# Three feed forwards: the down projection by seven products of halves, with the sums of weight blocks on GpSimd

## The chip, the core and the metric

The program runs on one core of one Trainium2 chip. The metric is the device time of one execution in microseconds (us), the median of several runs.

## What is computed

A sequence of 512 rows of width 1024 goes through three transformer layers in float32: one with a gated spatial branch and dilated attention, one with latent attention (MLA), one with an mLSTM. Each layer ends in a feed forward of width 4096 with a squared relu. The change concerns these three alone:

```python
n2 = rms_norm(h, norm_mlp_pre[l])                                        # first layer
hid = jnp.square(jax.nn.relu(jnp.einsum('bsd,df->bsf', n2, w_up[l])))    # 1024 -> 4096
mlp_out = jnp.einsum('bsf,fd->bsd', hid, w_down[l])                      # 4096 -> 1024
h = h + rms_norm(mlp_out, norm_mlp_post[l])
...
x = x + sqrelu_mlp(rms_norm_2(x, norm_ffn[i]), ffn_w1[i], ffn_w2[i])     # second and third
```

## The kernel before

**Products in three parts.** TensorE takes float32 operands in a rounded format (`fp32r`). So each operand x is split: a high part (ScalarE's `ACT.Copy` into an `fp32r` tile) and a low part (VectorE: x minus high). The helper `mm3` (L74 to L79) makes each product of two tiles with three matmuls of 512 columns: high by high, high by low, low by high.

**Units of weights.** All weights stream through the core as a list of units, each 128 partitions x up to 2048 float32 (1 MB), in an order that `plan_units` fixes. A unit lands in one of two slots of `raw_weights`; ScalarE makes its high part in one of two slots of `weights_hi`, VectorE its low part in `weights_lo`. The slots are held by three rules, all semaphores: a load waits for the low part of the unit two before it (`w_lo`), a high part waits for its load and for TensorE to be done with the unit two before (`gemm` against `release`), and TensorE waits for the low part.

**The feed forward** (`ffn`, L1415 on) goes through 4096 hidden columns in 8 chunks of 512. In a chunk TensorE makes 4 hidden tiles from 2 units of up weights (`ups`): a tile is 128 hidden columns x 512 rows, 8 parts of the depth x 3 = 24 matmuls into one bank of PSUM. ScalarE takes each tile through relu (L1563), square (L1565) and the high part (L1567); VectorE makes the low part (L1658). Then `downs`: for each half d of the 1024 output columns, one unit of down weights (512 x 512), 4 row tiles x 4 parts x 3 = 48 matmuls, and VectorE adds the 4 banks onto the accumulator (L1667). The order on each engine is written by hand; chunks 1 to 6 are a hardware loop on every engine. In the last chunk the row tiles 0 and 1 are finished first, so that the norm that follows can begin under the matmuls of tiles 2 and 3. In the first feed forward the accumulator is in `scratch` and its rows are scaled and normed on ScalarE, VectorE and, two pieces of 512 columns, GpSimd (L1473); in the others it is the residual itself. On VectorE a split's low part is L1650 in a feed forward and L328 elsewhere, on ScalarE the high part is L1556 and L322.

```python
for d in range(2):
    lo(dve, i, 2 + d)      # low part of a down unit
    summed(i, d)           # four additions out of PSUM
```

## Time and profile before

| | before |
|---|---|
| device time, median of 3 runs | 1998.15 us (1997.90 to 1998.96) |
| span of the profiled execution | 1996.8 us |
| TensorE busy, matmuls | 1981.8 us (99%), 9874 matmuls |
| VectorE busy | 941.2 us (47%) |
| ScalarE busy | 841.1 us (42%) |
| GpSimd busy | 50.0 us (3%) |

The results list no device time of its own for the profiled execution; its span, from the first to the last instruction, stands 1.35 us below the median of the runs, so what lies around the span is about a microsecond. A group of instructions in the profile is all instructions of one line, engine and shape. Busy time of TensorE counts overlapping matmuls once, so 374 ns for one matmul is not its pace: the pace is read from one start to the next.

### The profile page before, as it was taken

The page shows a single profiled execution, that of the slowest core. Times are in us where ns is not written, and L with a number is a line of the kernel's source. Part 1 is how long each engine was busy: PE and PEld are TensorE (multiplying, and loading weights), DVE is VectorE, ACT ScalarE, POOL GpSimd, SP SyncE. Part 2 cuts the span into 40 slices and gives each one's busy share as a digit, 9 for nine tenths or more (in the row PEclk, how much of TensorE's full clock was granted, in tenths as well). Part 3 has the DMA queues.
Part 4 walks back from the last instruction along what each step waited for, and adds up shares of the span by engine and source line. Part 5 has one row for each costly group of instructions (what it writes and reads, how often), then busy time and mean ns, then how long its engine had stood idle before and what let it go on. Part 6 is the DMA issues. An engine that isn't in the chain of part 4 may idle for free.

```text
span 1996.8 us, 24478 instructions
## 1 busy us (share of the span) xinstructions
PE 1981.8 (99%) x9874; PEld 1683.2 (84%) x9874; DVE 941.2 (47%) x1325; ACT 841.1 (42%) x1211; POOL 50.0 (3%) x83
## 2 busy tenths in 40 slices
PE   8999999999999999999999999999999999999999
PEld 6889988889888888888889888888888888888887
DVE  5655553355443433677644434343543454344433
ACT  5333334236333333577745323333456543333332
POOL 1000000000000000010000000000000000000000
PEclk9999999999999999999999999999999999999999
DMA  7233322232333232221012332323232123232322
GB/s 241 75 103 84 92 87 95 100 115 75 106 105 95 94 105 84 68 69 54 22 48 83 103 105 85 105 86 103 65 109 81 64 85 102 88 101 88 105 97 75
DMA packets 163368, 182.07 MB, mean 91 GB/s; under 512 B 7681, under 2 KB 125014, under 8 KB 163162
## 3 DMA queue, kind: packets, MB, share of 16 engines
q1 hardware_dynamic: 160746, 176.67, 27.8%
q0 software_dynamic: 2528, 4.29, 0.8%
q8 instruction: 56, 0.92, 0.2%
q14 instruction: 22, 0.18, 0.0%
q10 hardware_dynamic: 16, 0.00, 0.0%
HBM read 175.62 MB, written 2.11 MB: 89 GB/s over the span
## 4 chain that ended last, share of the span: by engine, by line
PE 97%; DVE 1%; ACT 1%; DMA 1%; issue 0%; SPq 0%; POOL 0%; ACTq 0%
PE psum L77 29%; PE psum L79 29%; PE psum L78 29%; PE psum L2042 2%; PE psum L2020 2%; PE psum L2473 1%; PE psum L2030 1%; PE psum L480 1%; PE psum L1998 1%; PE psum L2456 0%; PE psum L920 0%; DMA raw_weights<-in_w_in_dram 0%; PE psum L891 0%; PE psum L912 0%; PE psum L901 0%; PE psum L889 0%
## 5 line engine op out<-in xcount | busy, mean ns | idle before, releaser
L77 PE MATMUL psum<-norm_T_hi,weights_hi 128*128 128x512 f32 (+1 forms) x1440 | 538.7, 374 | 0.1
L79 PE MATMUL psum<-norm_T_hi,weights_lo 128*128 128x512 f32 (+1 forms) x1440 | 533.5, 371 | 0.0
L78 PE MATMUL psum<-norm_T_lo,weights_hi 128*128 128x512 f32 (+1 forms) x1440 | 533.0, 370 | 0.0
L77 PE MATMUL psum<-weights_hi,act_T_hi 128*128 128x512 f32 (+1 forms) x912 | 353.6, 388 | 0.0
L79 PE MATMUL psum<-weights_hi,act_T_lo 128*128 128x512 f32 (+1 forms) x912 | 352.3, 386 | 0.0
L78 PE MATMUL psum<-weights_lo,act_T_hi 128*128 128x512 f32 (+1 forms) x912 | 352.3, 386 | 0.0
L1556 ACT ACTIVATE weights_hi<-raw_weights 128x2048 fp32r<-128x2048 f32 x92 | 175.7, 1910 | 343.5 <-PE psum L79 343.5
L79 PEld LDWEIGHTS psum<-norm_T_hi,weights_lo 128*128 128x128 f32 x1440 | 271.2, 188 | 47.0
L77 PEld LDWEIGHTS psum<-norm_T_hi,weights_hi 128*128 128x128 f32 x1440 | 271.3, 188 | 45.9 <-DVE weights_lo L328 0.4
L78 PEld LDWEIGHTS psum<-norm_T_lo,weights_hi 128*128 128x128 f32 x1440 | 271.4, 188 | 45.1
L1650 DVE TENSOR_TENSOR weights_lo<-raw_weights,weights_hi 128x2048 fp32r<-128x2048 f32 x92 | 210.9, 2292 | 110.1 <-ACT weights_hi L1556 110.1
L328 DVE TENSOR_TENSOR weights_lo<-raw_weights,weights_hi 128x2048 fp32r<-128x2048 f32 (+3 forms) x74 | 157.0, 2121 | 168.8 <-ACT weights_hi L322 168.7
L1658 DVE TENSOR_TENSOR act_T_lo<-scratch,act_T_hi 128x512 fp32r<-128x512 f32 x96 | 66.6, 693 | 318.5 <-ACT act_T_hi L1567 318.5
L79 PEld LDWEIGHTS psum<-weights_hi,act_T_lo 128*128 128x128 f32 x912 | 171.2, 188 | 33.9
L77 PEld LDWEIGHTS psum<-weights_hi,act_T_hi 128*128 128x128 f32 x912 | 171.2, 188 | 33.6 <-issue 0.3
L78 PEld LDWEIGHTS psum<-weights_lo,act_T_hi 128*128 128x128 f32 x912 | 171.2, 188 | 33.2
L1563 ACT ACTIVATE scratch<-psum 128x512 f32<-128x512 f32 x96 | 57.3, 597 | 273.7 <-PE psum L79 273.7
L322 ACT ACTIVATE weights_hi<-raw_weights 128x2048 fp32r<-128x2048 f32 (+3 forms) x74 | 131.0, 1770 | 69.9 <-PE psum L79 69.8
L77 PE MATMUL psum<-weights_hi,norm_T_hi 128*128 128x512 f32 (+3 forms) x352 | 127.8, 363 | 0.8 <-DVE norm_T_lo L522 0.5
L78 PE MATMUL psum<-weights_lo,norm_T_hi 128*128 128x512 f32 (+3 forms) x352 | 125.5, 357 | 0.0
L79 PE MATMUL psum<-weights_hi,norm_T_lo 128*128 128x512 f32 (+3 forms) x352 | 125.5, 357 | 0.0
L1667 DVE TENSOR_TENSOR residual<-psum,residual 128x512 f32<-128x512 f32 x112 | 76.5, 691 | 103.3 <-PE psum L79 103.3
(293 smaller groups left out, 1794.5 us busy)
## 6 DMA issues: line engine op xcount, KB each, us to landing
raw_weights<-in_ffn_w_dram SPq DMA_DIRECT2D x64, 1024.0 KB, 5.2
raw_weights<-in_w_up_dram SPq DMA_DIRECT2D x16, 1024.0 KB, 5.5
raw_weights<-in_w_down_dram SPq DMA_DIRECT2D x16, 1024.0 KB, 5.1
raw_weights<-in_w_in_dram SPq DMA_DIRECT2D x26, 512.0 KB, 5.1
raw_weights<-in_w_in_dram SPq DMA_DIRECT2D x11, 1024.0 KB, 5.2
raw_weights<-in_mlstm_w_in_dram SPq DMA_DIRECT2D x8, 1024.0 KB, 5.1
raw_weights<-in_w_in_dram SPq DMA_DIRECT2D x24, 256.0 KB, 3.3
raw_weights<-in_w_out_dram SPq DMA_DIRECT2D x4, 1024.0 KB, 5.0
```

The costliest lines, as they stand in the source:

```text
L77: pe.matmul(out, ah, bh, start=start, stop=False)
L78: pe.matmul(out, ah, bl, start=False, stop=False)
L79: return pe.matmul(out, al, bh, start=False, stop=stop)
L322: act.activation(WH[:, u % 2, 0:c], RAW[:, u % 2, 0:c], ACT.Copy).then_inc(w_hi, 1)
L328: dve.tensor_tensor(WL[:, u % 2, 0:c], RAW[:, u % 2, 0:c], WH[:, u % 2, 0:c].bitcast(F32), SUB).then_inc(w_lo, 1)
L1556: act.activation(WH[:, u % 2, :], RAW[:, u % 2, :], ACT.Copy).then_inc(w_hi, 1)
L1563: act.activation(HS[:, f, :], PS[:, up_banks[f], :], ACT.Relu).then_inc(fr.sem, 1)
L1650: dve.tensor_tensor(WL[:, u % 2, :], RAW[:, u % 2, :], WH[:, u % 2, :].bitcast(F32), SUB).then_inc(w_lo, 1)
L1658: dve.tensor_tensor(AL[:, f, :], HS[:, f, :], AH[:, f, :].bitcast(F32), SUB).then_inc(fl.sem, 1)
L1667: dve.tensor_tensor(z, PS[:, banks[t], :], z, ADD).then_inc(acc.sem, 1)
L2020: pe.matmul(PS[:, b, c:c + w], QT[:, n % 2, t * P:t * P + P], KT[:, n % 2, 0:w], start=True, stop=True).then_inc(sc.sem, 1)
L2042: mm = pe.matmul(PS[:, 6, t * MV1:t * MV1 + MV1], PT[:, off[t] + j * P:off[t] + j * P + P], VN[:, n // 4 % 2, j, n % 4, :], start=j == 0, ...
```

## The change

The down projection of a chunk is a product of two 2 x 2 block matrices. Chunks are now 1024 hidden columns wide, 4 in a feed forward. A has the hidden values, split into rows 0 to 255 and 256 to 511 and into the even and the odd hidden tiles; B has the down weights of the same chunk, split in the same way by hidden tiles and into the two halves of the output columns. The block product is made as by Strassen and Winograd with seven products instead of eight:

- The sums of A: S1 = A21 + A22, S2 = S1 - A11, S3 = A11 - A21, S4 = A12 - S2. VectorE makes them tile by tile from each pair of hidden tiles (`first_tile`, `second_tile`); ScalarE makes their high and VectorE their low parts (`sums_hi`, `sums_lo`).
- The sums of B: T1 = B12 - B11, T2 = B22 - T1, T3 = B22 - B12, T4 = B21 - T2 up to sign. GpSimd makes them, four operations of 128 x 2048 per chunk, 48 in all (`weight_sum`), in the order T1, T3, T2, T4 (in the text sum 1 to sum 4), in place in the raw slots. Raw weights have four slots, two of them in `scratch`.
- The products P1 to P7, each 2 row tiles x 4 x 3 = 24 matmuls, with a unit of weights of its own. Their results stay in PSUM where the next product adds to them (`BEHIND`: a product starts on a bank when VectorE has added the bank's present value to the accumulator), so that after each product VectorE adds its two banks to one place of the accumulator, and the partial sums come out as wanted.

A chunk has 11 units: 4 of up weights, for 8 hidden tiles, and 7 for the products. The pace of units is unchanged in the up part (48 matmuls each) and twice as fast in the products (24 each). The loops over chunks are written out in full. Small things follow: some parameters have other places in `scratch`, and the last two row tiles of the residual are finished right half first (`by_end`).

The core of the diff:

```diff
-FCH = 512
+FCH = 1024
 NF = FF // FCH
...
+PRODUCTS = {"P1": ("A11", "W", True, 0, 0), "P5": ("S1", "V", True, 1, 1), "P6": ("S2", "W", False, 0, 1),
+            "P2": ("A12", "Y", True, 0, 0), "P7": ("S3", "W", False, 1, 1), "P3": ("S4", "V", False, 0, 1),
+            "P4": ("A22", "W", False, 1, 0)}
+INNER = ("P1", "P5", "P6", "P2", "P7", "P3", "P4")
+LAST = ("P1", "P5", "P6", "P2", "P3", "P7", "P4")
+BEHIND = {"P6": "P1", "P7": "P6", "P4": "P7", "P3": "P5"}
...
+            slots = (3, b, 2, a) if i % 2 else (a, b, 2, 3)
...
+            for j in range(4):
+                up_unit(j)
+            order = LAST if i == NF - 1 else INNER
+            for what in order:
+                if what == "P1":
+                    block_unit(0, 0, slots[0])
+                elif what == "P5":
+                    sum_unit(1, slots[3])
+                elif what == "P6":
+                    sum_unit(3, slots[0])
+                elif what == "P2":
+                    block_unit(1, 0, slots[3])
+                elif what == "P7":
+                    sum_unit(2, slots[1])
+                elif what == "P3":
+                    block_unit(1, 1, slots[2])
+                else:
+                    sum_unit(4, slots[0])
+            chunks[name].append(Chunk(slots, order, d[i][0][:, :, 512:1024]))
+        sums[0] += 4
...
+            @block.gpsimd
+            def _(pool):
+                def weight_sum(i, nth):
+                    ch, v = parts[i], u0 + 11 * i
+                    r0, r1, r2, r3 = (raw(s) for s in ch.slots)
+                    at_p = {what: v + 4 + p for p, what in enumerate(ch.order)}
+                    n0 = units[at_p["P5"]].summed - 1
+                    if nth == 1:
+                        pool.wait_ge(w_ld[ch.slots[0]], ld_total[at_p["P1"]])
+                        pool.wait_ge(w_ld[ch.slots[1]], beside_total[name, i])
+                        pool.wait_ge(w_lo, v + 4)
+                        pool.tensor_tensor(r3, r1, r0, SUB).then_inc(w_sum, 1)
+                    elif nth == 2:
+                        pool.wait_ge(w_ld[ch.slots[2]], ld_total[at_p["P3"]])
+                        pool.wait_ge(w_sum, n0 + 1)
+                        pool.tensor_tensor(r1, r2, r1, SUB).then_inc(w_sum, 1)
+                    elif nth == 3:
+                        pool.wait_ge(w_lo, at_p["P1"] + 1)
+                        pool.tensor_tensor(r0, r2, r3, SUB).then_inc(w_sum, 1)
+                    else:
+                        pool.wait_ge(w_ld[ch.slots[3]], ld_total[at_p["P2"]])
+                        pool.wait_ge(w_lo, at_p["P6"] + 1)
+                        pool.tensor_tensor(r0, r3, r0, SUB).then_inc(w_sum, 1)
+                for i in range(NF):
+                    for nth in range(1, 5):
+                        weight_sum(i, nth)
...
+                def product(i, p, between=None):
+                    what = parts[i].order[p]
+                    u = u0 + 11 * i + 4 + p
+                    stands, place, begins, _, _ = PRODUCTS[what]
+                    pe.wait_ge(w_lo, u + 1)
+                    for t in range(2):
+                        if t and between:
+                            between()
+                        if what in BEHIND:
+                            pe.wait_ge(*taken(i, parts[i].order.index(BEHIND[what]), t))
+                        elif place == "Y":
+                            pe.wait_ge(fr.sem, fr.at(8 * i + 4 + t + 1))
+                        elif i:
+                            pe.wait_ge(*taken(i - 1, parts[i - 1].order.index("P4" if place == "W" else "P3"), t))
+                        for k in range(4):
+                            if t == 0 and what == "P1":
+                                pe.wait_ge(fl.sem, fl.at(16 * i + 4 * k + 1))
+                            elif t == 0 and k == 3:
+                                pe.wait_ge(fl.sem, fl.at(16 * i + 12 + {"S1": 2, "S2": 2, "A12": 3, "A22": 3, "S3": 4, "S4": 4}[stands]))
+                            w = slice(512 * k, 512 * k + 512)
+                            mm = mm3(pe, PS[:, bank_of[place][t], :], *rows(stands, k, t), WH[:, u % 2, w], WL[:, u % 2, w],
+                                     begins and k == 0, k == 3, not begins)
                         mm.then_inc(gemm, 1)
...
+                def hidden(i, f):
+                    n = 4 * i + f // 2
+                    h = H[:, n % 2, f % 2, :]
+                    act.wait_ge(gemm, tile_done(i, f))
+                    if f % 2 == 0 and n >= 2:
+                        act.wait_ge(fl.sem, fl.at(4 * (n - 2) + 4))
+                    act.activation(h, PS[:, up_banks[f % 4], :], ACT.Relu).then_inc(fr.sem, 1)
+                    act.wait_ge(fr.sem, fr.at(8 * i + f + 1))
+                    act.activation(h, h, ACT.Square).then_inc(fs.sem, 1)
+                    act.wait_ge(fs.sem, fs.at(8 * i + f + 1))
+                    if f % 2:
+                        act.activation(A2H[:, f // 2, :], h, ACT.Copy).then_inc(fh.sem, 1)
+                    else:
+                        act.activation(A1H[:, f // 2, :], h[:, 0:256], ACT.Copy).then_inc(fh.sem, 1)
+                def sums_hi(i, j):
+                    n = 4 * i + j
+                    for b in range(2):
+                        act.wait_ge(summed.sem, summed.at(4 * n + 3 + b))
+                        act.activation(SH[:, j, 2 * b:2 * b + 2, :], ST[:, 2 * b:2 * b + 2, :], ACT.Copy).then_inc(fh.sem, 1)
 
...
+                    for j in range(4):
+                        hidden(i, 2 * j)
+                        if i == j == 0:
+                            split_hi(act, v + 2)
+                        if j == 3:
+                            split_hi(act, v + 5)
+                        hidden(i, 2 * j + 1)
+                        if j < 3 and i + j:
+                            split_hi(act, v + 2 + j)
+                        sums_hi(i, j)
+                    if i < NF - 1:
+                        for p in range(1, 7):
+                            split_hi(act, v + 5 + p)
...
+                def first_tile(i, j):
+                    n = 4 * i + j
+                    h = H[:, n % 2, 0, :]
+                    dve.wait_ge(fs.sem, fs.at(8 * i + 2 * j + 1))
+                    if n:
+                        dve.wait_ge(fl.sem, fl.at(4 * n))
+                    dve.tensor_tensor(ST[:, 2, :], h[:, 0:256], h[:, 256:512], SUB).then_inc(summed.sem, 1)
+                    dve.wait_ge(fh.sem, fh.at(4 * n + 1))
+                    dve.tensor_tensor(A1L[:, j, :], h[:, 0:256], A1H[:, j, :].bitcast(F32), SUB).then_inc(fl.sem, 1)
+                def second_tile(i, j):
+                    n = 4 * i + j
+                    a, b = H[:, n % 2, 0, :], H[:, n % 2, 1, :]
+                    dve.wait_ge(fs.sem, fs.at(8 * i + 2 * j + 2))
+                    dve.tensor_tensor(ST[:, 0, :], a[:, 256:512], b[:, 256:512], ADD).then_inc(summed.sem, 1)
+                    dve.wait_ge(summed.sem, summed.at(4 * n + 2))
+                    dve.tensor_tensor(ST[:, 1, :], ST[:, 0, :], a[:, 0:256], SUB).then_inc(summed.sem, 1)
+                    dve.wait_ge(summed.sem, summed.at(4 * n + 3))
+                    dve.tensor_tensor(ST[:, 3, :], b[:, 0:256], ST[:, 1, :], SUB).then_inc(summed.sem, 1)
+                def second_lo(i, j):
+                    n = 4 * i + j
+                    dve.wait_ge(fh.sem, fh.at(4 * n + 2))
+                    dve.tensor_tensor(A2L[:, j, :], H[:, n % 2, 1, :], A2H[:, j, :].bitcast(F32), SUB).then_inc(fl.sem, 1)
+                def sums_lo(i, j, b):
+                    dve.wait_ge(fh.sem, fh.at(16 * i + 4 * j + 3 + b))
+                    s = slice(2 * b, 2 * b + 2)
+                    dve.tensor_tensor(SL[:, j, s, :], ST[:, s, :], SH[:, j, s, :].bitcast(F32), SUB).then_inc(fl.sem, 1)
+                def add(i, p, t):
+                    what = parts[i].order[p]
+                    _, place, _, r, d = PRODUCTS[what]
+                    dve.wait_ge(gemm, product_done(i, p, t))
+                    z, src = acc_half(d, 2 * r + t), PS[:, bank_of[place][t], :]
+                    if gain is not None and i == 0 and what in ("P1", "P5", "P6", "P4"):
+                        dve.tensor_copy(z, src).then_inc(acc.sem, 1)
...
+                    for j in range(4):
+                        first_tile(i, j)
+                        if i == j == 0:
+                            split_lo(dve, v + 2)
+                        if j == 3:
+                            split_lo(dve, v + 5)
+                        second_tile(i, j)
+                        if j == 3:
+                            sums_lo(i, j, 0)
+                            second_lo(i, j)
+                            sums_lo(i, j, 1)
+                            continue
+                        second_lo(i, j)
+                        if i + j:
+                            split_lo(dve, v + 2 + j)
+                        sums_lo(i, j, 0)
+                        sums_lo(i, j, 1)
+                    for p in range(7 if i < NF - 1 else 3):
+                        if p:
+                            split_lo(dve, v + 5 + p)
+                        for t in range(2):
+                            add(i, p, t)
+                i = NF - 1
```

**What the order of the instructions shows.** VectorE in the middle of the up part. Before, a turn of the loop has two low parts of weights and four of hidden tiles between them:

```order
L1650 TENSOR_TENSOR weights_lo<-raw_weights,weights_hi 128x2048 [waits weights_hi_made]
L1657 REGISTER_ALU
L1658 TENSOR_TENSOR act_T_lo<-scratch,act_T_hi 128x512 [waits hidden_hi]
L1657 REGISTER_ALU
L1658 TENSOR_TENSOR act_T_lo<-scratch,act_T_hi 128x512 [waits hidden_hi]
L1649 REGISTER_ALU
L1650 TENSOR_TENSOR weights_lo<-raw_weights,weights_hi 128x2048 [waits weights_hi_made]
```

Now, from the third pair of hidden tiles of a chunk to the first tile of the fourth (`feed_operands` holds the high and low parts of A11, A12 and A22, `act_T` those of the four sums; L412 is a weight's low part, here P1's):

```order
L1827 TENSOR_TENSOR scratch<-scratch 128x256 [waits hidden_lo,square_made]
L1829 TENSOR_TENSOR feed_operands<-scratch,feed_operands 128x256 [waits hidden_hi]
L1836 TENSOR_TENSOR scratch<-scratch 128x256 [waits square_made]
L1838 TENSOR_TENSOR scratch<-scratch 128x256 [waits hidden_sums]
L1840 TENSOR_TENSOR scratch<-scratch 128x256 [waits hidden_sums]
L1845 TENSOR_TENSOR feed_operands<-scratch,feed_operands 128x512 [waits hidden_hi]
L412 TENSOR_TENSOR weights_lo<-scratch,weights_hi 128x2048 [waits weights_hi_made]
L1850 TENSOR_TENSOR act_T_lo<-scratch,act_T_hi 128x512 [waits hidden_hi] x2
L1827 TENSOR_TENSOR scratch<-scratch 128x256 [waits hidden_lo,square_made]
L1829 TENSOR_TENSOR feed_operands<-scratch,feed_operands 128x256 [waits hidden_hi]
```

What was one operation per tile is four per tile, and the low part that TensorE wants for the last quarter of P1 is the last row.

VectorE in the down part, before:

```order
L1650 TENSOR_TENSOR weights_lo<-raw_weights,weights_hi 128x2048 [waits weights_hi_made]
L1662 ISA
L1667 TENSOR_TENSOR scratch<-psum,scratch 128x512 [waits gemm_groups_done]
L1662 REGISTER_ALU
L1667 TENSOR_TENSOR scratch<-psum,scratch 128x512 [waits gemm_groups_done]
L1662 REGISTER_ALU
L1667 TENSOR_TENSOR scratch<-psum,scratch 128x512 [waits gemm_groups_done]
L1662 REGISTER_ALU
L1667 TENSOR_TENSOR scratch<-psum,scratch 128x512 [waits gemm_groups_done]
L1649 REGISTER_ALU
L1650 TENSOR_TENSOR weights_lo<-raw_weights,weights_hi 128x2048 [waits weights_hi_made]
```

and now, with P6's low part the first L412, then P2's, P7's and P3's:

```order
L1860 TENSOR_TENSOR scratch<-psum,scratch 128x512 [waits gemm_groups_done] x2
L412 TENSOR_TENSOR weights_lo<-scratch,weights_hi 128x2048 [waits weights_hi_made]
L1860 TENSOR_TENSOR scratch<-psum,scratch 128x512 [waits gemm_groups_done]
L1860 TENSOR_TENSOR key_rows<-psum,key_rows 128x512 [waits gemm_groups_done]
L412 TENSOR_TENSOR weights_lo<-raw_weights,weights_hi 128x2048 [waits weights_hi_made]
L1860 TENSOR_TENSOR scratch<-psum,scratch 128x512 [waits gemm_groups_done] x2
L412 TENSOR_TENSOR weights_lo<-raw_weights,weights_hi 128x2048 [waits weights_hi_made]
L1860 TENSOR_TENSOR scratch<-psum,scratch 128x512 [waits gemm_groups_done] x2
L412 TENSOR_TENSOR weights_lo<-scratch,weights_hi 128x2048 [waits weights_hi_made]
```

A weight's low part stands behind every two additions, where it stood behind every four.

GpSimd had nothing inside a chunk. Now it has, from one chunk into the next (`weights_landed` are the loads, `weights_lo_made` the low parts, by which it knows that a raw slot is free):

```order
L1611 TENSOR_TENSOR raw_weights<-raw_weights,scratch 128x2048 [waits weights_lo_made,weights_landed1,weights_landed3]
L1615 TENSOR_TENSOR raw_weights<-scratch,raw_weights 128x2048 [waits weight_sums_made,weights_landed2]
L1618 TENSOR_TENSOR scratch<-scratch,raw_weights 128x2048 [waits weights_lo_made]
L1622 TENSOR_TENSOR scratch<-raw_weights,scratch 128x2048 [waits weights_lo_made,weights_landed0]
L1611 TENSOR_TENSOR scratch<-raw_weights 128x2048 [waits weights_lo_made,weights_landed1,weights_landed0]
```

## Rows read from the trace of the kernel before

**Rows 1.** The page: busy times, and the chain that ended last

```profile
PE 1981.8 (99%) x9874; PEld 1683.2 (84%) x9874; DVE 941.2 (47%) x1325; ACT 841.1 (42%) x1211; POOL 50.0 (3%) x83
...
PE 97%; DVE 1%; ACT 1%; DMA 1%; issue 0%; SPq 0%; POOL 0%; ACTq 0%
PE psum L77 29%; PE psum L79 29%; PE psum L78 29%; PE psum L2042 2%; PE psum L2020 2%; PE psum L2473 1%; PE psum L2030 1%; PE psum L480 1%; PE psum L1998 1%; PE psum L2456 0%; PE psum L920 0%; DMA raw_weights<-in_w_in_dram 0%; PE psum L891 0%; PE psum L912 0%; PE psum L901 0%; PE psum L889 0%
```

**Rows 2.** Waits of TensorE: total us, times, longest us

```profile
PE psum L620 <- DMA ident<-in_c_ident_dram: 6.6, 1, 6.6
PE psum L480 <- DVE scratch L437: 1.7, 1, 1.7
...
PE psum L77 <- DVE weights_lo L328: 0.2, 1, 0.2
```

**Rows 3.** Timeline, first feed forward: start us, us, engine, operation [idle before]

```profile
565.01 0.39 PE L77 MATMUL psum<-norm_T_hi,weights_hi 128*128 128x512 f32 x1
...
565.21 1.92 ACT L1556 ACTIVATE weights_hi<-raw_weights 128x2048 fp32r<-128x2048 f32 x1 [8.96 <-PE psum L79]
...
567.16 2.29 DVE L1650 TENSOR_TENSOR weights_lo<-raw_weights,weights_hi 128x2048 fp32r<-128x2048 f32 x1 [1.26 <-ACT weights_hi L1556]
...
570.45 0.39 PE L77 MATMUL psum<-norm_T_hi,weights_hi 128*128 128x512 f32 x1
...
570.65 0.60 ACT L1563 ACTIVATE scratch<-psum 128x512 f32<-128x512 f32 x1 [3.52 <-PE psum L79]
...
571.28 0.63 ACT L1565 ACTIVATE scratch<-scratch 128x512 f32<-128x512 f32 x1
...
571.94 0.63 ACT L1567 ACTIVATE act_T_hi<-scratch 128x512 fp32r<-128x512 f32 x1
...
572.61 0.69 DVE L1658 TENSOR_TENSOR act_T_lo<-scratch,act_T_hi 128x512 fp32r<-128x512 f32 x1 [3.15 <-ACT act_T_hi L1567]
...
608.73 1.92 ACT L1556 ACTIVATE weights_hi<-raw_weights 128x2048 fp32r<-128x2048 f32 x1 [8.96 <-PE psum L79]
```

**Rows 4.** The page's groups: xcount | busy us, mean ns | idle

```profile
L1556 ACT ACTIVATE weights_hi<-raw_weights 128x2048 fp32r<-128x2048 f32 x92 | 175.7, 1910 | 343.5 <-PE psum L79 343.5
...
L1650 DVE TENSOR_TENSOR weights_lo<-raw_weights,weights_hi 128x2048 fp32r<-128x2048 f32 x92 | 210.9, 2292 | 110.1 <-ACT weights_hi L1556 110.1
```

**Rows 5.** Timeline of VectorE, two operations of 256 columns

```profile
928.11 0.43 DVE L2217 TENSOR_TENSOR scratch<-scratch 128x256 f32<-128x256 f32 x1
928.46 0.42 DVE L2218 TENSOR_TENSOR scratch<-scratch 128x256 f32<-128x256 f32 x1
```

**Rows 6.** One turn of the loop: its us, busy TensorE, loads, VectorE, ScalarE, GpSimd

```profile
612.55:656.07 43.52, 43.52 (x193) 36.04 (x193) 17.40 (x17) 14.90 (x16) 0.00 (x0) 1.00 0.30 96
```

**Rows 7.** Loads of the up projection's weights, from issue to landing

```profile
DMA to landing us min/median/max: 5.3/5.5/6.6
```

**Rows 8.** GpSimd's two-input operations (ns min/median/max), timelines of it and VectorE

```profile
L1473 POOL TENSOR_TENSOR scratch<-scratch x2: 1286/2105/2924, 822.1 to 823.3; 128x512 f32<-128x512 f32 x2
L2184 POOL TENSOR_TENSOR scratch<-scratch x2: 2737/2742/2747, 930.2 to 968.9; 128x1536 f32<-128x1536 f32 x2
...
822.06 4.19 POOL L1473 TENSOR_TENSOR scratch<-scratch 128x512 f32<-128x512 f32 x2 [500.66 <-DVE scratch L1696]
...
821.22 1.28 DVE L1696 TENSOR_TENSOR scratch<-psum,scratch 128x512 f32<-128x512 f32 x2
822.58 2.51 DVE L328 TENSOR_TENSOR weights_lo<-raw_weights,weights_hi 128x1664 fp32r<-128x1664 f32 x1
...
829.81 1.89 DVE L328 TENSOR_TENSOR weights_lo<-raw_weights,weights_hi 128x1664 fp32r<-128x1664 f32 x1 [1.31 <-ACT weights_hi L322]
```

**Rows 9.** Two stretches ending the first feed forward, as in rows 6

```profile
806.00:815.00 9.00, 9.00 (x41) 7.47 (x40) 6.16 (x8) 3.83 (x7) 0.00 (x0) 1.00 0.32 95
815.00:822.00 7.00, 7.00 (x32) 5.80 (x31) 5.16 (x8) 2.90 (x7) 0.00 (x0) 1.00 0.01 2
```

**Rows 10.** Span and mean granted clock of the core

```profile
core 0: 1996.8 us, clock 1.000
```

505 lines of the change are left out of this document (255 added, 250 removed).

## The prediction

> **What bounds the kernel now.** I read the page first: TensorE is busy for 1981.8 of 1996.8 us and the chain that ended last lies on it for 97%, almost all of it in the three matmuls of the product helper [rows 1]. Then the waits of TensorE: one for a transfer at the start (6.6 us), one of 1.7 us, and the whole list holds nothing else of over 1.1; behind the split of a weight it waited 0.2 us in all [rows 2]. So the kernel is a queue of matmuls without holes. The reader is to see that fewer matmuls pay in full, as long as nothing that replaces them opens a hole.
>
> The pace is in the timeline of one turn of the loop of a feed forward [rows 3]. A hidden tile, 24 matmuls, begins at 565.01 and the next at 570.45: 5.44 us. The splits of weights by ScalarE stand at 565.21 and 608.73 at the same place of two turns, 43.52 us for 192 matmuls: **0.2267 us a matmul**. The same rows give the reaction times: ScalarE begins 0.20 us after TensorE's next tile does, each step that follows a step of another engine begins 0.03 us after its end. Durations: high half of 2048 columns 1.91, low half 2.29, relu 0.60, square and copy 0.63, VectorE on 512 columns 0.69 [rows 3, 4]; a 256-column operation of VectorE 0.42, and one straight behind another begins 0.08 us before the record of the first ends [rows 5]. In a whole turn VectorE is busy 17.4 of 43.5 us and GpSimd 0 [rows 6].
>
> **What is removed.** Each product of halves is 2 row tiles x 4 x 3 = 24 matmuls. A chunk of 1024 hidden columns has seven in place of eight, and there are 4 chunks x 3 feed forwards: 12 x 24 = 288 matmuls, 288 x 0.2267 = **-65.3 us**. All of it lies on the bound engine. A chunk is now 192 + 168 = 360 matmuls, 81.6 us.
>
> **What is added beside it.** Per chunk VectorE has 11 low halves (25.2 us), 14 additions (9.7) and for each of four pairs of hidden tiles 5 operations of 256 and 3 of 512 columns (4.2 each, 16.7): 51.6 of 81.6 us. ScalarE: 11 x 1.91 + 8 x 1.23 + 4 x 0.42 (taken as VectorE's 256-column row) + 12 x 0.63 = 40.1 us. Both fit. The loads are as many bytes as before; each has its slot free at least 5 us ahead of use and lands in 5.3 to 6.6 us [rows 7], and the tightest, P2's, is issued when P5 is split and sum 3 is made and is needed some 7 us later: nothing. The loops are written out, so there are more instructions to fetch; stages written out already show no wait of TensorE for that above the few in rows 2: nothing, at most 2 us.
>
> **What one sum on GpSimd costs.** The 48 sums of 128x2048 have no row. Nearest are two of 512 columns and two of 1536 [rows 8]. The first of 512 took 1.29 us; 1536 took 2.74, with one tensor as both inputs. A line through both gives 3.5 us at 2048, four times the first gives 5.1. I take **4.4**, a little over the middle, because the row with two different inputs, as here, is the nearer in kind. The Trainium skill (GPSIMD Engine Reference, Performance versus the Vector engine) has 4497 ns for a `tensor_tensor` of 2048 fp32 columns, a size that no row of this trace has; by that figure the total below would be 5 us higher.
>
> **What it does to VectorE.** The same rows show that the two engines don't run side by side. While GpSimd's first 512 ran (822.06 to 823.35), VectorE's split of 1664 columns began at 822.58 and took 2.51 us; it takes 1.89 alone. Its end, 825.09, is 823.20 + 1.89: it stood still until GpSimd was nearly done. GpSimd's second 512 took 2.92 and ended at 826.25 (822.06 + 4.19), 1.16 us after that split's end. VectorE's operations with one input from PSUM show no such loss. So I count: an operation of VectorE with both inputs in SBUF and a sum exclude each other, and a sum of h us holds it for h - 0.15.
>
> **Where that opens holes**, in an inner chunk with tile 0 at time 0. GpSimd's sum 1 waits for the split of the fourth up unit, sum 3 for P1's, sum 4 for P6's and P2's load.
> - Tile 3 ends at 21.76; +0.2, relu, square, copy, high half, low half: the fourth unit is split at 28.0. Until VectorE has made the low half of A11's last quarter it has 12 more operations (two sums' low halves, the six of pair 2, P1's split, two more low halves, the difference and the low half of tile 6): 8.7 us less the overlaps, 8.3 with own waits. Each finds its input early enough. Sums 1, 2 and 3 fall into this stretch one after another, since each is released by then. 28.0 + 8.3 + 3 x 4.25 = 49.1, with GpSimd's gaps 49.6. P1's fourth quarter is due at 8 x 5.44 + 9 x 0.2267 = 45.6: **hole of 4.0**, growing by 3 us per us of h.
> - From there VectorE has P5's split, the three sums of pair 3, three low halves, two additions and P6's split, ending at 58.9; TensorE is done with P5 at 58.5: **0.5**. In the list it is the additions that stand ahead of the split.
> - Sum 4 begins at 59.0 and ends at 63.4. P2's split stands behind it and ends at 65.6; P6 ends at 64.5: **1.1**, growing by 1 per us of h.
> - P7, P3 and P4: high half, low half and the reaction are 4.4 us against 5.44 of the product in between: no hole.
>
> Sum: 5.7 us a chunk, or 4h - 11.85. x 12 = 69.0. In the first chunk of each feed forward the first four tiles end 2.7 us apart, which I count with 1.1 more (3.4). The last chunks put the norm's work between four splits where before there were two; VectorE was busy 11.3 of 16 us there [rows 9], so 0 to 5, taken as 2. **+74.4 - 65.3 = +9.1 us.** The span of the profiled execution, 1996.8, becomes 2005.9; the runs' median lies 1.35 above that span, and I keep the distance: **2007**.
>
> **The rivals.**
> - *A, the forecast*: the sums push VectorE aside, the holes cost more than a product saves. Its own range by h from 4.2 to 5.14: 0 to +45, 1998 to 2043. For it: 822.58. Against it: that is one meeting of the two. Chance 0.50.
> - *B, the other side, the same mechanism with short sums*: at h = 3.5 a chunk loses 2.15, together 25.8 + 3.4 + 2 = 31.2, so -34 and 1964. The two balance where 12 x (4h - 11.85) = 59.9, at **h = 4.2**. For it: the 1536 row, at 1.79 ns a column where 4.4 us stands for 2.15. Chance 0.30.
> - *C, no exclusion*: the two engines run side by side, as before's split could have been late for another reason. Left are 0.5 a chunk and the ends, 6 + 3 + 2 = 11: -54, 1944. Against it: the end times above fit to 0.1 us from both sides. Chance 0.10.
> - *D, TensorE's clock*: the granted clock of before is 1.000 in the mean [rows 10], but after its start TensorE never stood for over 1.7 us [rows 2], and now it would for 4 us in each chunk. No row is at the lower of the two levels, 1.2 GHz; at half the clock a product takes 5.44 us more. Half a product's worth in each chunk is +33, 2040; a whole one +65. Chance 0.10. The Trainium skill (TensorE: Matmul & The Clock Gate, The HAM clock gate) says that an idle engine falls to 1.2 GHz and comes back when busy; by that rule D is likelier than I make it, and no row here decides.
>
> **How the numbers follow.** A measurement of this kernel can tell 0.2%, 4 us, from no change. A gives slower 0.42 and within 0.2% 0.08; B faster 0.28, within 0.02; C faster 0.10; D slower 0.10. Together faster 0.38, same 0.10, slower 0.52. The time is A's, 2007. The range reaches from 1955, below B's 1964 by the uncertain ends, to 2045, A's upper end: outside are C and the longer half of D and a little of A, under 0.2.
>
> **What would show it.** In the profile of the changed kernel: 288 fewer matmuls; 48 GpSimd operations of 128x2048 with a duration between 3.5 and 5.1 us when unblocked (decides A or B, at 4.2); low halves of 2.29 us that sometimes last 6; TensorE waiting 12 times for `feed_operands` (A11's last low half) for some 4 us and, for about 1 us each, for low weights before P2 (INNER's fourth) and 0.5 before P6; GpSimd's records reaching over 7 us where VectorE was first. No wait of TensorE behind P7, P3, P4, none for a transfer. Wrong: if low halves stay at 2.29 beside GpSimd (C), if the granted clock of the feed forwards falls below 1.00 (D), or if the largest wait is behind ScalarE or a load.

## The result, and the profile after

| | before | after |
|---|---|---|
| device time, median | 1998.14 us (1997.90 to 1998.96) | **2025.22 us** (2021.43 to 2027.05) |
| ratio | | **1.0132**, 95% interval 1.0118 to 1.0146 |
| span of the profiled execution | 1996.8 us | 2022.6 us |
| mean granted clock of TensorE | 1.000 | 0.986 |

The change makes the kernel 27 us slower. It was to give 65.3 us back, so some 92 us were lost elsewhere; of the profiled execution, which is 25.8 longer than the one before, 91.1. The page first: busy times, and the chain that ended last. They answer to [rows 1].

```profile
PE 1950.9 (96%) x9586; PEld 1643.1 (81%) x9586; DVE 1292.5 (64%) x1625; ACT 950.1 (47%) x1343; POOL 284.3 (14%) x131
...
PE 76%; DVE 18%; ACT 5%; issue 1%; DMA 0%; DVEq 0%; ACTq 0%
```

The 288 matmuls are gone (9874 to 9586), yet TensorE's busy time fell by only 31 us. The chain, which lay on TensorE for 97%, now lies on VectorE for 18%. The waits of TensorE, as in [rows 2]:

```profile
PE psum L96 <- DVE feed_operands L1829: 45.1, 12, 4.2
PE psum L96 <- DVE weights_lo L412: 10.2, 17, 1.2
PE psum L711 <- DMA ident<-in_c_ident_dram: 6.4, 1, 6.4
PE psum L564 <- DVE scratch L521: 2.0, 1, 2.0
```

Twelve waits for A11's last low half, one in each chunk, and shorter ones for low weights: the holes that the prediction placed. Next GpSimd and VectorE over P1 in the second chunk of the first feed forward (start us, us, engine, line; two excerpts):

```profile
596.56 5.73 DVE L1850 TENSOR_TENSOR act_T_lo<-scratch,act_T_hi 128x512 fp32r<-128x512 f32 x2
596.82 4.93 POOL L1611 TENSOR_TENSOR raw_weights<-raw_weights,scratch 128x2048 f32<-128x2048 f32 x1 [52.61 <-DVE weights_lo L412]
601.89 4.93 POOL L1615 TENSOR_TENSOR raw_weights<-scratch,raw_weights 128x2048 f32<-128x2048 f32 x1
602.40 4.71 DVE L1827 TENSOR_TENSOR scratch<-scratch 128x256 f32<-128x256 f32 x1
...
611.42 5.66 DVE L1850 TENSOR_TENSOR act_T_lo<-scratch,act_T_hi 128x512 fp32r<-128x512 f32 x2
...
617.52 0.42 DVE L1829 TENSOR_TENSOR feed_operands<-scratch,feed_operands 128x256 fp32r<-128x256 f32 x1
```

```profile
611.58 4.94 POOL L1618 TENSOR_TENSOR scratch<-scratch,raw_weights 128x2048 f32<-128x2048 f32 x1 [4.76 <-DVE weights_lo L412]
627.79 4.62 POOL L1622 TENSOR_TENSOR scratch<-raw_weights,scratch 128x2048 f32<-128x2048 f32 x1 [11.27 <-DVE weights_lo L412]
```

Two low halves of 512 columns, 0.69 us each, last 5.73 beside sum 1; a difference of 256 columns, 0.42 us, lasts 4.71 beside sum 2. Each sum of the three pushes VectorE once, by 4.3 to 4.5 us, in the order that the prediction gave. Sums 1 to 3 show 4.93 and 4.94: each began under a running operation of VectorE (sum 1 at 596.82, VectorE's first low half, 0.69 long, until 597.25), and its record is 0.3 longer than that of the fourth. That one, with nobody in its way, took **4.62**; the figure of the Trainium skill that the prediction named, 4497 ns, is 3% below it. VectorE's additions with one input in PSUM are not pushed: their groups have 685 to 689 ns in the mean, as without a sum.

TensorE over the same hole and what comes behind it:

```profile
614.01 0.40 PE L98 MATMUL psum<-weights_hi,feed_operands 128*128 128x512 f32 x1
618.00 0.50 PE L96 MATMUL psum<-weights_hi,feed_operands 128*128 128x512 f32 x1 [3.58 <-DVE feed_operands L1829]
618.33 0.39 PE L97 MATMUL psum<-weights_lo,feed_operands 128*128 128x512 f32 x1
...
619.88 0.63 PE L97 MATMUL psum<-weights_lo,feed_operands 128*128 128x512 f32 x1
620.31 0.63 PE L98 MATMUL psum<-weights_hi,feed_operands 128*128 128x512 f32 x1
620.73 0.63 PE L96 MATMUL psum<-weights_hi,feed_operands 128*128 128x512 f32 x1
...
622.87 0.44 PE L98 MATMUL psum<-weights_hi,feed_operands 128*128 128x512 f32 x1
623.14 0.40 PE L96 MATMUL psum<-weights_hi,act_T_hi 128*128 128x512 f32 x1
```

3.99 us between two starts, a hole of 3.76. Then the second loss: from 619.88 to 622.87 matmuls start every 0.43 us in place of 0.23. Windows before and in that stretch (columns as in [rows 6]) show why:

```profile
608.00:620.00 12.00, 8.41 (x37) 6.56 (x36) 11.86 (x9) 6.35 (x9) 4.94 (x1) 0.98 0.01 2
620.00:623.00 3.00, 3.00 (x9) 2.32 (x8) 2.69 (x7) 1.15 (x2) 0.00 (x0) 0.51 0.51 136
```

The granted clock is 0.51, the lower of the two levels (1.2 GHz), with TensorE busy throughout. Here TensorE stood still for 3.6 us, worked on for 1.5 to 1.9 us at the full pace, and then had some 3 us at the low clock. That happened in 11 of 12 chunks, not always at the same moment: in six of them the first start behind the hole is already slow (0.59 us to the next), and the full pace was back 2.7 to 6.1 us after TensorE had begun again.

The one other chunk, the last of the first feed forward, kept its clock (1.00 from 796 to 808) behind a hole of 3.75; why, no run shows. Its wait before P2 is the longest of all, 1.37 beyond the pace, where the others have 0.6:

```profile
809.77 0.39 PE L98 MATMUL psum<-weights_hi,act_T_lo 128*128 128x512 f32 x1
811.37 0.50 PE L96 MATMUL psum<-weights_hi,feed_operands 128*128 128x512 f32 x1 [1.21 <-DVE weights_lo L412]
```

The balance of the profiled execution, from the starts of the matmuls in all 12 chunks, each time what a start is later than the pace of 0.2267:

| | forecast | measured |
|---|---|---|
| hole before P1's last quarter | 12 x 4.0 | 12 x 3.9 = 47.2 |
| first chunks, before P1 | 3.4 | 3 x 1.4 = 4.2 |
| hole before P6 | 12 x 0.5 | 0 |
| hole before P2 | 12 x 1.1 | 11 x 0.6 + 1.4 = 7.9 |
| last chunks and other | 2 | 3.5 |
| slow matmuls behind P1's holes (low clock) | (rival D) | **22.6** |
| pace of matmuls that read `feed_operands`: 0.2333 | - | 864 x 0.0066 = 5.7 |
| sum | 74.4 | 91.1 |

Of the 22.6 some 1.2 are no matter of the clock: the second start behind a hole comes 0.33 after the first at the full clock too, 0.1 late. "Other" is what remains; in it are one wait of 1.7 us for the residual in a last chunk and 1.3 of such second starts before P2. The split between the small rows is good to 1 us.

### The profile page after: what moved, and what is told of

Its sections match the earlier page's. It is cut to its first block, busy times and chain, and to the rows that moved or that the text cites. A ratio compares the mean times of both kernels' runs of the same rounds, so it can differ in the third digit from the quotient of the medians.

```text
span 2022.6 us, 23527 instructions
## 1 busy us (share of the span) xinstructions
PE 1950.9 (96%) x9586; PEld 1643.1 (81%) x9586; DVE 1292.5 (64%) x1625; ACT 950.1 (47%) x1343; POOL 284.3 (14%) x131
## 4 chain that ended last, share of the span: by engine, by line
PE 76%; DVE 18%; ACT 5%; issue 1%; DMA 0%; DVEq 0%; ACTq 0%
PE psum L96 22%; PE psum L98 22%; PE psum L97 22%; DVE act_T_lo L1850 7%; DVE weights_lo L412 6%; DVE scratch L1827 3%; ACT weights_hi L406 3%; PE psum L2241 2%; PE psum L2219 1%; PE psum L2672 1%; PE psum L2229 1%; PE psum L564 1%; PE psum L2197 1%; ACT scratch L1724 0%; PE psum L2655 0%
## 5 line engine op out<-in xcount | busy, mean ns | idle before, releaser
L412 DVE TENSOR_TENSOR weights_lo<-raw_weights,weights_hi 128x2048 fp32r<-128x2048 f32 (+3 forms) x136 | 308.0, 2264 | 213.3 <-ACT weights_hi L406 213.1
L406 ACT ACTIVATE weights_hi<-raw_weights 128x2048 fp32r<-128x2048 f32 (+3 forms) x136 | 249.7, 1836 | 219.8 <-PE psum L98 219.8
L96 PE MATMUL psum<-weights_hi,act_T_hi 128*128 128x512 f32 (+1 forms) x528 | 204.2, 387 | 0.0
L98 PE MATMUL psum<-weights_hi,act_T_lo 128*128 128x512 f32 (+1 forms) x528 | 203.1, 385 | 0.0
L97 PE MATMUL psum<-weights_lo,act_T_hi 128*128 128x512 f32 (+1 forms) x528 | 203.1, 385 | 0.0
L412 DVE TENSOR_TENSOR weights_lo<-scratch,weights_hi 128x2048 fp32r<-128x2048 f32 x66 | 160.2, 2428 | 57.2 <-ACT weights_hi L406 57.2
L406 ACT ACTIVATE weights_hi<-scratch 128x2048 fp32r<-128x2048 f32 x66 | 126.2, 1913 | 127.4 <-PE psum L98 127.4
L96 PE MATMUL psum<-weights_hi,feed_operands 128*128 128x512 f32 x288 | 126.1, 438 | 54.9 <-DVE feed_operands L1829 45.1
L1850 DVE TENSOR_TENSOR act_T_lo<-scratch,act_T_hi 128x512 fp32r<-128x512 f32 x96 | 169.2, 1794 | 2.9 <-ACT act_T_hi L1735 2.9
L97 PE MATMUL psum<-weights_lo,feed_operands 128*128 128x512 f32 x288 | 122.3, 424 | 0.0
```

Of the source, the lines that this page charges most:

```text
L96: pe.matmul(out, ah, bh, start=start, stop=False, skip_group_check=more)
L97: pe.matmul(out, ah, bl, start=False, stop=False, skip_group_check=more)
L98: return pe.matmul(out, al, bh, start=False, stop=stop, skip_group_check=more)
L406: act.activation(WH[:, u % 2, 0:c], raw(units[u].slot)[:, 0:c], ACT.Copy).then_inc(w_hi, 1)
L412: dve.tensor_tensor(WL[:, u % 2, 0:c], raw(units[u].slot)[:, 0:c], WH[:, u % 2, 0:c].bitcast(F32), SUB).then_inc(w_lo, 1)
L1850: dve.tensor_tensor(SL[:, j, s, :], ST[:, s, :], SH[:, j, s, :].bitcast(F32), SUB).then_inc(fl.sem, 1)
```

## The experiments

The theory after the result: (1) each sum shuts VectorE's operations with two inputs in SBUF out, three times in P1's stretch, and that alone makes the holes; (2) the holes, not GpSimd, bring the clock down. Rivals: the longer program or the new order of products is slow by itself; GpSimd slows VectorE by writing; the clock falls from GpSimd's or the whole chip's load. The kernels of each group ran on one chip beside the kernel before (1998.0 to 1998.5).

**e1: sums without length.** The four weight sums are cut to 8 columns; the rest of each is left out of the computation.

```diff
-                        pool.tensor_tensor(r3, r1, r0, SUB).then_inc(w_sum, 1)
+                        pool.tensor_tensor(r3[:, 0:8], r1[:, 0:8], r0[:, 0:8], SUB).then_inc(w_sum, 1)
```

> Each of the 48 sums on GpSimd is cut to 8 of its 2048 columns; the other 2040 columns of every weight sum are left out, all waits stay. Theory 1 (a sum of 4.6 us holds VectorE off, that opens the holes of TensorE, and the holes bring its clock down): the holes before P1's last quarter (3.76 us each) and before P2 (0.6) go, the granted clock is 1.00 in the feed forwards, and what stays is the slower pace with operands from feed_operands (4 to 6 us in all), the ends and up to 0.5 us a chunk of VectorE's own order: 1998 - 65 + 8 to 16 = 1941 to 1949 us. Rival 1 (the holes come from VectorE's own longer list and not from GpSimd): holes of 3 to 4 us stay at the same place, 2010 to 2025 us. Rival 2 (the clock falls in the feed forwards for another reason than the holes): holes gone, but matmuls at 0.43 us remain, some 25 us more: 1966 to 1974.

1945.88 us (ratio 0.9738, 0.9721 to 0.9754), clock 1.000, no hole before P1's last quarter or before P2. All but some 13 of the 65 us come back, and the low clock goes with the holes. Of the 13, 5.7 are the slower pace and 4.7 the one wait that a chunk has left: 0.4 us before P6, for P6's low part. It is the forecast's 0.5, and the same in e4, from which these rows are:

```profile
614.31 0.39 PE L98 MATMUL psum<-weights_hi,act_T_lo 128*128 128x512 f32 x1
614.81 0.19 PEld L96 LDWEIGHTS psum<-weights_hi,act_T_hi 128*128 128x128 f32 x1 [0.54 <-DVE weights_lo L412]
614.81 0.50 PE L96 MATMUL psum<-weights_hi,act_T_hi 128*128 128x512 f32 x1
```

**e2: GpSimd writes only.** Three fills of the whole target in place of each sum, 5.4 us of GpSimd together; the weight sums are left out.

```diff
-                        pool.tensor_tensor(r3, r1, r0, SUB).then_inc(w_sum, 1)
+                        long_write(pool, r3)
...
+                    for _ in range(2):
+                        pool.memset(z, 0.0).then_inc(wr.sem, 1)
...
+                    pool.memset(z, 0.0).then_inc(w_sum, 1)
```

> Each sum on GpSimd is replaced by three fills of the same 128x2048 block one after another: GpSimd only writes and reads nothing; the weight sums are left out. If the three fills take 4.5 us or more together, theory 1 in the form that GpSimd's reads exclude VectorE's operations with two inputs in SBUF gives low parts of 0.69 and 2.29 us beside them, no holes and 1941 to 1952 us. Rival (any work of GpSimd on SBUF holds VectorE off, or a long wait for the semaphore of a sum is what delays): holes as in the changed kernel, 2010 to 2030. If the fills are much shorter than 4.5 us, the run tells only about VectorE's durations beside them.

1946.18 us (0.9739, 0.9723 to 0.9755). The group of the low halves that lasted 5.7 in pairs:

```profile
L1858 DVE TENSOR_TENSOR act_T_lo<-scratch,act_T_hi 128x512 fp32r<-128x512 f32 x96 | 62.8, 686 | 2.9 <-ACT act_T_hi L1743 2.9
```

686 ns in the mean, where the same group in the changed kernel has 1794. GpSimd is busy longer than with the sums and VectorE doesn't notice.

**e7: GpSimd reads one tensor.** Each sum becomes a copy of one of its inputs; the weight sums are left out.

```diff
-                        pool.tensor_tensor(r3, r1, r0, SUB).then_inc(w_sum, 1)
+                        pool.tensor_copy(r3, r1).then_inc(w_sum, 1)
```

> Weight sums are left out: in place of each GpSimd makes a copy of one of its two inputs, 128 x 2048, by one tensor_copy; P5, P6, P7 and P4 take those values. GpSimd reads one tensor and writes one. Theory (GpSimd's reads of SBUF hold VectorE's two-input operations, however many inputs): low parts of 512 and 2048 columns beside a copy last longer than their 0.69 and 2.29 us by up to the copy's time, and the time lies above the 1946 of the version without long sums if a copy is over about 3 us. Rival (only GpSimd's operations with two inputs hold VectorE): low parts keep 687 and 2291 ns in the mean, no hole over 0.3 us, 1946.

One execution: 1945.84 us. By the time alone the rival would stand, but a copy takes only 1.90 us with nobody in its way, too short to open a hole. VectorE and GpSimd in the first feed forward decide:

```profile
587.78 2.98 DVE L1850 TENSOR_TENSOR act_T_lo<-scratch,act_T_hi 128x512 fp32r<-128x512 f32 x2
588.02 2.20 POOL L1611 COPY raw_weights<-raw_weights 128x2048 f32<-128x2048 f32 x1 [53.90 <-DVE weights_lo L412]
590.35 2.17 POOL L1615 COPY raw_weights<-scratch 128x2048 f32<-128x2048 f32 x1
590.87 1.94 DVE L1827 TENSOR_TENSOR scratch<-scratch 128x256 f32<-128x256 f32 x1
```

Two low halves last 2.98 in place of 1.3, a difference of 256 columns 1.94 in place of 0.42: pushed by one copy each. So one read is enough, and writes alone (e2) push nothing. The Trainium skill (SBUF — State Buffer, Who interferes with whom) has it so: a VectorE instruction with two SBUF inputs contends with a GpSimd instruction that reads SBUF, not with one that only writes. e2 and e7 agree.

**e3: shorter sums.** 1792 of 2048 columns (the last 256 of each weight sum are left out), to measure the slope.

```diff
-                        pool.tensor_tensor(r3, r1, r0, SUB).then_inc(w_sum, 1)
+                        pool.tensor_tensor(r3[:, 0:1792], r1[:, 0:1792], r0[:, 0:1792], SUB).then_inc(w_sum, 1)
```

> Each sum on GpSimd is cut to 1792 of 2048 columns; 256 columns of every weight sum are left out. A sum should take 0.55 us less (4.07). Theory 1: the hole before P1's last quarter shrinks by three times that, from 3.76 to 2.1 us, and the one before P2 goes nearly, by 0.55. If the clock falls only after long holes, matmuls at 0.43 us are rare and the time is 1972 us; if it falls after holes of 2 us as often as after 4, 1997. Rival (the hole is not made of the three sums one after another): it shrinks by 0.55 or less, and the time stays above 2010.

1988.86 us (0.9951, 0.9934 to 0.9967), clock 0.995. The waits of TensorE:

```profile
PE psum L96 <- DVE feed_operands L1829: 28.6, 12, 3.6
PE psum L96 <- DVE weights_lo L412: 4.9, 9, 0.7
```

Sum 4 takes 4.07 or 4.11 in the mean, 0.55 less, and the hole of an inner chunk goes from 3.76 to 2.12: a slope of 3.0, the forecast's. The clock now fell in only 5 chunks: in all 3 first ones, where the hole is 3.8, and in 2 of the 9 with 2.1. The hole before P2 did not nearly go, as was expected: it is 0.8 in the seven chunks that kept their clock, which is 0.55 less than the 1.4 of the changed kernel's one such chunk, and not to be seen in the other five.

**e5: one of the three pushes gone.** VectorE makes sum 3 itself, in its own order behind P1's low part. The whole computation.

```diff
-                    for nth in range(1, 5):
+                    for nth in (1, 2, 4):
                         weight_sum(i, nth)
...
+                def third_sum(i):
...
+                    dve.tensor_tensor(r0, r2, r3, SUB).then_inc(w_sum, 1)
...
                         sums_lo(i, j, 1)
+                        if j == 2:
+                            third_sum(i)
```

> The whole computation; GpSimd makes the sums 1, 2 and 4, and VectorE makes sum 3 itself (2.2 us) after the second tile pair's successor, behind the split of P1's unit. Theory (each GpSimd sum of 4.62 us ahead of A11's last low half pushes VectorE by 4.45): the three pushes of the stretch become two and an operation of 2.2, so the hole before P1's last quarter goes from 3.76 to about 1.5 us; the hole before P2 stays at 0.6 to 1.1. The clock: with holes of 1.5 it falls in few chunks (with 2.1 us it fell in 2 of 9), so 0.99 to 1.00. Time 1946 + 12 x (1.5 + 0.8) = 1974, with 5 either way. Rival 1 (the hole comes from GpSimd's work of the whole chunk, not of this stretch): a quarter less work, a quarter less hole, some 2.9 us, clock fallen in half of the chunks, about 2000. Rival 2 (the clock falls by itself in this arrangement whatever the hole): granted clock 0.986, about 1998.

1983.72 us (0.9928, 0.9913 to 0.9943), 10 above the theory's number, with clock 1.000. The waits:

```profile
PE psum L96 <- DVE weights_lo L412: 18.6, 16, 1.3
PE psum L96 <- DVE feed_operands L1836: 16.1, 12, 1.7
```

The hole before P1's last quarter is 1.4 in an inner chunk, as said, and none of 12 brought the clock down. Most of the miss is P2: 1.4 a chunk where 0.8 was counted. At full clock TensorE is at P2 some 2 us earlier than in the changed kernel, so it meets the whole wait behind sum 4. In the changed kernel the low clock hid part of that wait, which is why its share there is 0.6 in eleven chunks; in the one that kept its clock it is 1.4 as here. The rest of the miss are the first chunks, with 1.4 before P1 and 1.9 before its last quarter. There is no hole before P6, here or in the changed kernel: TensorE comes later by the hole ahead, and that covers the 0.4 of e1 and e4.

**e4: no sum on GpSimd.** VectorE makes all four, where it has time: sums 1 and 2 behind the second pair of tiles, 3 behind the third pair, 4 between two splits. The whole computation.

```diff
+                        if j == 1:
+                            weight_sum(i, 1)
+                            weight_sum(i, 2)
+                        if j == 2:
+                            weight_sum(i, 3)
...
+                        if p == 3:
+                            weight_sum(i, 4)
```

> The whole computation; the four sums of a chunk are made by VectorE (2.29 us each, 2.2 behind one another) and not by GpSimd, the first two behind the low part of the fourth up unit, the third behind the sums of the third pair of tiles, the fourth behind P2's low part. Theory 1: VectorE gives 9.2 us of its own a chunk instead of being held for up to 18; the stretch that ended 3.76 us late gets 3 x (4.45 - 2.2) = 6.7 us shorter, so the hole before P1's last quarter is gone, holes of 0 to 1.2 us before P6 or P2 stay, the clock stays at 1.00: 1942 to 1956 us. Rival (VectorE is the bound engine by its load): 60.8 of 81.6 us a chunk plus waits don't fit, holes of 2 us and more, 1970 to 2000.

**1946.18 us** (0.974, 0.9723 to 0.9756), clock 1.000, as fast as e1, where the sums are absent. A sum costs VectorE 2.29 us, half of GpSimd's, and it pushes nobody. So the sevenfold product does pay 52 us once its sums are on the engine that has the time and makes them twice as fast.

**e6: the hole without GpSimd.** The version e4, with P1's last quarter waiting for one low part more. The whole computation, later.

```diff
-                                pe.wait_ge(fl.sem, fl.at(16 * i + 4 * k + 1))
+                                pe.wait_ge(fl.sem, fl.at(16 * i + 4 * k + (2 if k == 3 else 1)))
```

> The whole computation, with the sums on VectorE, no sum on GpSimd; the only edit to that version: the last quarter of P1 waits for one more step of VectorE and ScalarE (the low parts of S1 and S2's pair instead of the low part of A11's last quarter), which leaves TensorE standing once in each of 12 chunks. Theory (the clock falls because TensorE stood still, whatever GpSimd does): holes of 2 to 5 us, 12 of them; where they are over 3.5 us the granted clock falls behind nearly all (some 0.985 in the mean) and the time is 1946 + 12 x hole + some 25 us, 2030 for holes of 4.9. Rival (the clock fell in the changed kernel by GpSimd's activity or by the slot of the program, not by the hole): clock stays 1.000 and the time is 1946 + 12 x hole, 2005 for holes of 4.9.

2019.03 us (1.0104, 1.0089 to 1.012). First the wait, then TensorE in a chunk, then windows around and in it:

```profile
PE psum L96 <- DVE act_T_lo L1847: 53.7, 12, 4.5
```

```profile
616.72 0.79 PE L96 MATMUL psum<-weights_hi,feed_operands 128*128 128x512 f32 x1 [4.47 <-DVE act_T_lo L1847]
617.31 0.63 PE L97 MATMUL psum<-weights_lo,feed_operands 128*128 128x512 f32 x1
...
621.15 0.50 PE L97 MATMUL psum<-weights_lo,feed_operands 128*128 128x512 f32 x1
621.48 0.40 PE L98 MATMUL psum<-weights_hi,feed_operands 128*128 128x512 f32 x1
```

```profile
618.00:621.00 3.00, 3.00 (x8) 2.32 (x8) 0.69 (x1) 0.00 (x0) 0.00 (x0) 0.50 0.31 119
608.00:622.00 14.00, 9.53 (x33) 7.32 (x32) 7.50 (x11) 4.81 (x6) 0.00 (x0) 0.76 0.22 77
```

With GpSimd idle (0.00) the clock falls to 0.50 behind the hole, in 12 chunks of 12. The holes are 4.64 each, 55.7 us, and the slow matmuls behind them add 22.5; that is 5.3 more than the 72.9 by which e6 stands above e4, 4.7 of them the waits before P6 of e4 that are gone here. The theory holds, the rival (GpSimd's activity) falls. The time is 11 below the 2030 expected: 3 since a hole of 4.9 between starts is one of 4.64, 5 by the waits before P6, and 2.5 since the slow matmuls cost less than the 25 taken.

Put together, the chunks of four kernels, by how long TensorE stood (starts beyond the pace):

| hole, us | kernel | clock fell in |
|---|---|---|
| 1.4 to 1.9 | e5 | 0 of 12 |
| 2.1 | e3, inner chunks | 2 of 9 |
| 3.8 | after, inner; e3, first | 11 of 12 |
| 4.4 | after, first chunks | 3 of 3 |
| 4.6 | e6 | 12 of 12 |

**e8: the slower pace.** The down matmuls, which read `feed_operands`, go at 0.2333 us; others at 0.2267. Here the kernel *before*, whole, with the high and low parts of the hidden tiles of the second and third feed forward in that region.

```diff
+            HH, HL = (AH, AL) if gain is not None else (FO[:, 4096 + 2048 * n:6144 + 2048 * n].rearrange("p (k s) -> p k s", k=4) for n in range(2))
...
-                        mm = mm3(pe, PS[:, bank, :], AH[:, f, tt], AL[:, f, tt],
+                        mm = mm3(pe, PS[:, bank, :], HH[:, f, tt], HL[:, f, tt],
```

> The whole computation of the kernel before, in its order, with eight products of halves; the only edit: in the second and third feed forward the high and low parts of the hidden tiles lie in the other region of the memory, where the changed kernel has the operands of its down products, and two small tables move out of the way. Theory (the pace of 0.2333 instead of 0.2268 us that the changed kernel's down matmuls have comes from that place): 1536 down matmuls at 0.2333, + 10 us, 2008. Rival (the pace comes from the order of the three matmuls, the products' banks or the writing into another bank, not from the place): 1998.5, within 1 us, and the down matmuls at 0.2268.

2008.32 us (1.0051, 1.0037 to 1.0065), the pace 0.2334: the place alone makes it. In the compiled program the region begins at byte 154560 of each partition, 960 past a multiple of 1024; the tiles of all other operands begin 128 past one. Four versions of e4 tell height from remainder (each the whole computation; one unused tensor ahead of the region, or the region and scratch declared ahead of the residual):

```diff
+        sb("gap", [P, 16])
         with nc.sbuf_tensor("feed_operands", [P, 8192], F32R) as FO:
```

> The whole computation, the version with the sums on VectorE; the only edit: 64 unused bytes per partition ahead of the region of the down products' operands, so that it begins at a multiple of 128 bytes (154624) as the other operands' tiles do, where before it began 64 bytes past one (154560). Theory (TensorE's pace of 0.2333 us for operands that lie there comes from the odd 64 bytes): the 72 matmuls of a chunk that read them go at 0.2268, 864 x 0.0066 = 5.7 us less, 1940.5. Rival (the pace comes from where in the memory the region lies, or from tiles of other shape): 1946.2, pace 0.2333.

> The whole computation, the version with the sums on VectorE; the region of the down products' operands and scratch trade places with the residual, so that the operands begin at byte 131200, a multiple of 128 and lower in the memory. Theory (the odd 64 bytes make the pace): 0.2268 here too, 1940.5, as with the gap. Rival (how high in the memory the region lies makes it): the gap alone changes nothing, 1946.2, and only this one gains. Second rival (neither): both stay at 1946.2.

> The whole computation: the version with the operands' region moved below the residual, with 64 unused bytes per partition ahead of the region, so that it begins at byte 131264 in place of 131200. Theory 1 (how high the region lies makes the pace): nothing changes, pace 0.2266, 1941.7. Theory 2 (the start's remainder makes it: all operands of other matmuls begin at 128 past a multiple of 1024, the slow region at 960 past one, the region moved at 128 past one): pace back to 0.2326 to 0.2333, 1945 to 1947.

> The whole computation: the version with the sums on VectorE, the region where it was but with 192 unused bytes ahead of it, so that it begins at byte 154752, 128 past a multiple of 1024. Theory 1 (height): the pace stays at 0.2326 to 0.2333, 1945 to 1946.2. Theory 2 (the remainder): pace 0.2266, 1941.7.

| | begins at byte | past a multiple of 1024 | pace | time |
|---|---|---|---|---|
| e4 | 154560 | 960 | 0.2335 | 1946.18 |
| e9, gap of 64 | 154624 | 0 | 0.2326 | 1944.97 |
| e12, gap of 192 | 154752 | 128 | 0.2266 | **1941.74** |
| e10, moved | 131200 | 128 | 0.2266 | 1941.69 |
| e11, moved and 64 | 131264 | 192 | 0.2335 | 1945.87 |

The first theory of e9 (a multiple of 128 bytes is enough) fell: its gap gave a seventh of the gain in pace, and 1.2 of the 4.4 us in time. The height fell with e11 and e12. What holds is the remainder: with the region's start in step with the others', 128 past a multiple, the pace is full. TensorE's first matmuls of P1 in e4:

```profile
603.47 0.40 PE L96 MATMUL psum<-weights_hi,feed_operands 128*128 128x512 f32 x1
603.71 0.39 PE L97 MATMUL psum<-weights_lo,feed_operands 128*128 128x512 f32 x1
603.94 0.40 PE L98 MATMUL psum<-weights_hi,feed_operands 128*128 128x512 f32 x1
```

and in e12:

```profile
603.11 0.39 PE L96 MATMUL psum<-weights_hi,feed_operands 128*128 128x512 f32 x1
603.34 0.39 PE L97 MATMUL psum<-weights_lo,feed_operands 128*128 128x512 f32 x1
603.57 0.39 PE L98 MATMUL psum<-weights_hi,feed_operands 128*128 128x512 f32 x1
```

Which modulus counts (256, 512 or 1024 bytes would all fit these five starts), and whether it is the start itself or its distance from the other operand's, stays open. e12 is the best version that computes everything: 2.8% faster than the kernel before (0.9716, 0.9700 to 0.9733), 4.1% faster than the changed one.

## Why the prediction was right or wrong

- **The direction and its mechanism**: right. Slower, because GpSimd's sums push VectorE aside and holes open in TensorE where they were placed. e1, e4, e5 show it from three sides: without the sums, or with them elsewhere, these holes go or shrink. Rival B (short sums) fell with 4.62 us, above its balance of 4.2; rival C (no exclusion) fell with the pairs of low halves of 5.7 us.
- **h**: taken 4.4, measured 4.62. The line through the two sizes (3.5) was misleading, presumably since its larger one had a single tensor as both inputs (no run tells).
- **The sum of A**: 74.4 forecast, some 63 measured (47.2 + 4.2 + 7.9 + 3.5). With h = 4.62 its formula gives 6.6 a chunk. P1's hole came 0.9 shorter than that formula (3.76 for 4.0 + 3 x 0.22 = 4.66), although the slope of 3 is right (e3). From the fourth unit's split (596.8) to A11's last low half (617.9) it counts 22.2 us, and the rows have 21.1: the 0.5 of GpSimd's gaps is not there, the three pushes are 13.1 in place of 13.4, VectorE's own work 8.0 in place of 8.3. P6's hole was not there, hidden behind P1's. P2's was half in eleven chunks, since TensorE came late to it; at full clock it is 1.4 (e5), above the 1.1.
- **The step that failed is the clock**, a term put at nothing in the sum. The prediction set A and D against each other, with 0.50 and 0.10, and its 2007 held nothing for D. But D needs just the holes that A forecasts: given A's 4 us in each chunk, D follows, in 11 chunks of 12. Its price was near, half a product's worth a chunk, 33 us, against some 22 measured; its chance was not. What was lacking was a row with a hole of 4 us in a busy TensorE. The only one near, 6.6 us at the start of the program [rows 2], gives no warning: in the kernel before the granted clock reads 1.00 in it and behind it (columns as in [rows 6]):

```profile
6.00:9.00 3.00, 0.66 (x3) 0.60 (x4) 1.91 (x5) 1.63 (x5) 0.00 (x0) 1.00 1.03 353
9.00:15.00 6.00, 5.99 (x26) 5.05 (x25) 5.03 (x9) 5.86 (x12) 0.00 (x0) 1.00 1.05 393
```

  The rule of the Trainium skill on the clock gate, quoted there, stood on the right side, and e6 agrees with it. With D's 33 on top of A's 9 the forecast would have been 2040; with the measured sizes, the pace included, it is 2024. That the miss is only 18 us is luck in part: A's sum was 12 too high, and without that the 28 of the clock and the pace would have shown in full.
- **The slower pace** of 5.7 us was foreseen nowhere: a second term at nothing. No step asked where new operands lie.
- **What would show it**: the 288 matmuls, the 12 waits of some 4 us for `feed_operands`, one before P2 (0.6 in place of 1), none behind P7, P3 and P4, and none for a transfer all came; 0.5 before P6 and GpSimd's records of over 7 us did not. VectorE was never far enough ahead: the longest record of a sum is 5.09.

## What to carry to other kernels

Work given to GpSimd is not free of VectorE: in these runs an operation that reads SBUF there stopped VectorE's operations with both inputs in SBUF for nearly its whole length (4.3 to 4.5 of 4.62 us), so where VectorE feeds the bound engine, an operation of 2.3 us on VectorE is cheaper than one of 4.6 "beside" it. When a forecast opens holes of a few microseconds in TensorE, price the low clock behind each one in the same sum, as a consequence and not as a rival. And when two kernels do the same matmuls at paces that differ by a few per cent, look at the byte at which their operands begin.
